# Four edits to a two-layer transformer kernel on one core: transposes one place later, masks later, x in pieces, last norm on three engines

## The reference

```python
u = rms_norm(h, norm_pre_mix[l]);  proj = u @ w_in[l]          # q_sb k_sb v_sb q_lat kv_lat k_r gate_logits
y_sb  = stick_breaking_attention(q_sb, k_sb, v_sb) @ w_o_sb[l]
y_mla = mla_attention(...) @ w_o_mla[l]                        # from q_lat, kv_lat, k_r
mixed = (g_sb * y_sb + g_mla * y_mla) @ w_out[l]               # g: sigmoid(gate_logits + b_gate)
h = h + rms_norm(mixed, norm_post_mix[l])
gu = rms_norm(h, norm_pre_ffn[l]) @ w_gate_up[l]
h = h + rms_norm((silu(g) * up) @ w_down[l], norm_post_ffn[l])
# second block, twice (attention, then retention):
x = layer_norm(ALPHA * x + y, ln_gain[i], ln_bias[i])          # (x - mu) * rsqrt(var + eps) * gain + bias
```

## Time and profile before

| | us |
|---|---|
| median of 3 runs (lowest, highest) | 2512.87 (2512.11, 2513.63) |
| the profiled execution | 2515.63 |
| its span, first to last instruction | 2513.8 |
| TensorE busy (share of the span) | 2483.7 (99%) |
| VectorE busy | 1531.8 (61%) |
| ScalarE busy | 1215.9 (48%) |
| GpSimd busy | 14.9 (1%) |

### The profile page before, as it was taken

The page is one execution under the profiler, slowest core; times in us unless marked ns, Lnnn a source line. Parts: engine busy times, 40 slices in busy tenths (PEclk is TensorE's granted clock), DMA queues, the critical chain, the costliest instruction groups (busy, mean ns, idle before and its releaser), DMA issues.

```text
span 2513.8 us, 33162 instructions
## 1 busy us (share of the span) xinstructions
PE 2483.7 (99%) x11514; PEld 2074.0 (83%) x11514; DVE 1531.8 (61%) x2132; ACT 1215.9 (48%) x1538; POOL 14.9 (1%) x29
## 2 busy tenths in 40 slices
PE   8999999999999999999999999999999999999997
PEld 7889888878888888888888888887888888888886
DVE  5557666565744454455556787668766566666557
ACT  5455776544644444444445445653544444444442
POOL 0000000000000000000000000000000000000000
PEclk9999999999999999999999999999999999999999
DMA  7566566775566666666567455455656556565663
GB/s 263 174 193 185 171 189 176 235 254 191 176 207 189 187 192 185 191 186 191 193 194 250 119 182 181 134 195 178 197 154 198 172 171 185 174 182 169 224 192 136
DMA packets 215026, 472.19 MB, mean 188 GB/s; under 512 B 14944, under 2 KB 24208, under 8 KB 213904
## 3 DMA queue, kind: packets, MB, share of 16 engines
q1 hardware_dynamic: 205968, 447.54, 58.1%
q10 hardware_dynamic: 6944, 12.86, 1.5%
q0 software_dynamic: 2016, 10.53, 1.2%
HBM read 464.57 MB, written 6.29 MB: 187 GB/s over the span
## 4 chain that ended last, share of the span: by engine, by line
PE 90%; DVE 4%; DMA 3%; ACT 2%; issue 1%; SPq 0%; ACTq 0%; DVEq 0%
PE acc L461 25%; PE acc L463 25%; PE acc L462 25%; PE aux L461 4%; PE aux L463 4%; PE aux L462 4%; PE aux L482 1%; ACT whi L1104 1%; DVE wlo L1721 1%; DMA raw<-w_in 1%; DMA raw<-w_o_sb 1%; DVE h L2385 0%; DMA raw<-r_w_out 0%; DMA raw<-w_out 0%; DVE stats L2379 0%
## 5 line engine op out<-in xcount | busy, mean ns | idle before, releaser
L1721 DVE TENSOR_TENSOR wlo<-raw,whi 128x1024 fp32r<-128x1024 f32 x823 | 1001.4, 1224 | 879.5 <-ACT whi L1104 877.2
L1104 ACT ACTIVATE whi<-raw 128x1024 fp32r<-128x1024 f32 x823 | 868.7, 1060 | 1129.1 <-PE acc L463 832.8
L461 PE MATMUL acc<-whi,xh 128*128 128x512 f32 (+1 forms) x2288 | 896.5, 392 | 1.7 <-DVE wlo L1795 1.1
L463 PE MATMUL acc<-whi,xl 128*128 128x512 f32 (+1 forms) x2288 | 889.7, 389 | 0.0
L462 PE MATMUL acc<-wlo,xh 128*128 128x512 f32 (+1 forms) x2288 | 889.2, 389 | 0.0
L463 PEld LDWEIGHTS acc<-whi,xl 128*128 128x128 f32 x2288 | 430.0, 188 | 88.4
L461 PEld LDWEIGHTS acc<-whi,xh 128*128 128x128 f32 x2288 | 430.4, 188 | 87.6 <-DVE xl L1791 1.8
L462 PEld LDWEIGHTS acc<-wlo,xh 128*128 128x128 f32 x2288 | 430.6, 188 | 83.5
L461 PE MATMUL acc<-whi,osh 128*128 128x512 f32 x400 | 155.9, 390 | 0.3 <-DVE osl L1731 0.2
L461 PE MATMUL aux<-whi,osh 128*128 128x512 f32 x400 | 156.0, 390 | 0.0
L463 PE MATMUL aux<-whi,osl 128*128 128x512 f32 x400 | 155.7, 389 | 0.0
(11 more groups left out here) (400 smaller groups left out, 1945.5 us busy)
## 6 DMA issues: line engine op xcount, KB each, us to landing
raw<-r_w_in SPq DMA_DIRECT2D x188, 512.0 KB, 3.7
raw<-w_gate_up SPq DMA_DIRECT2D x172, 512.0 KB, 3.6
raw<-w_in SPq DMA_DIRECT2D x112, 512.0 KB, 4.0
raw<-w_down SPq DMA_DIRECT2D x84, 512.0 KB, 4.6
raw<-a_w_in SPq DMA_DIRECT2D x76, 512.0 KB, 3.7
raw<-r_w_out SPq DMA_DIRECT2D x60, 512.0 KB, 4.6
raw<-w_out SPq DMA_DIRECT2D x28, 512.0 KB, 4.7
raw<-a_w_out SPq DMA_DIRECT2D x28, 512.0 KB, 4.0
```

The lines of the kernel that those rows point to most:

```text
L461: pe.matmul(dst, lh, rh, start=start, stop=False, skip_group_check=True)
L463: return pe.matmul(dst, ll, rh, start=False, stop=stop, skip_group_check=True)
L1104: A(whi[:, slot], raw[:, slot], ACT.Copy).then_inc(hi_done, 1)
L1721: V.tensor_tensor(wlo[:, slot], raw[:, slot], f32(whi[:, slot]), ALU.subtract).then_inc(lo_done, 1)
```

## The change

1. TensorE transposes the scaled first chunk behind u = 7 of the second chunk instead of u = 5; the copies into `qkT` on ScalarE and VectorE move likewise.
2. POOL fetches the masks when `used` is 16 instead of 4.
3. x goes into `h` in eight pieces of 256 KB, each when `used` has reached a further third unit of the second half of the gates, after `sb_y` is 4. `gbc1` waits for `used` to reach the first unit of `out`. VectorE waits for all eight pieces.
4. In the last layer norm, tile 0: VectorE copies its scale into `scale0` and goes on to tile 1; ScalarE multiplies the four pieces by it, and GpSimd adds the bias row to each. SP stores tile 0 by the new count `result0`.

```diff
+        scale0 = put("scale0", [P, 1], F32)
@@ sync
-                sp.wait_ge(sem("result"), n + 1)
+                sp.wait_ge(sem("result" if t else "result0"), n % 4 + 1)
@@ gpsimd
-            pool.wait_ge(used, 4)
+            pool.wait_ge(used, 16)
             bring("masks", [(mask_raw[:, 0:P], c_ntri), (mask_raw[:, P:2 * P], c_nones),
                             (mask_raw[:, 2 * P:5 * P], c_mask_sb), (mask_raw[:, 5 * P:9 * P], c_mask_mla)])
+            pool.wait_ge(sem("sb_y"), 4)
+            for n in range(8):
+                t, cols = n // 4, slice(n % 4 * CW, (n % 4 + 1) * CW)
+                pool.wait_ge(used, UNITS["gate"] + 32 + 3 * n)
+                pool.dma_start(h[:, t, cols], x[t * P:(t + 1) * P, cols]).then_inc(sem("x_again"), 16)
+
             pool.wait_ge(sem("dve_stage"), DVE_STAGE["mla_end"])
-            pool.dma_start(h[:], x.rearrange("(t p) n -> p t n", p=P)).then_inc(sem("x_again"), 16)
-
+            pool.wait_ge(used, UNITS["out"])
             bring("gains_in", [(gbc1[:], g_post_mix.partition_broadcast(P))])
...
+            pool.wait_ge(sem("gains_in"), 96)
+            for b in range(4):
+                cols = slice(b * CW, (b + 1) * CW)
+                pool.wait_ge(sem("scaled"), b + 1)
+                nc.gpsimd.tensor_tensor(h[:, 0, cols], h[:, 0, cols], lng2[:, 1, cols], ALU.add).then_inc(sem("result0"), 1)
@@ tensor
-                        if (c == 1 and u == 5) if first else u == 3:
+                        if (c == 1 and u == 7) if first else u == 3:
                             turned("qkv", i * 2 + c - 1)
                             turn_blocks(s0, 4).then_inc(sem("qkv_tr"), 1)
@@ scalar
-                        if c == 1 and u == 5 and first:
+                        if c == 1 and u == 7 and first:
                             cp("qkv", flat(qkT[:, 0:2]), aux[:, 0], 0)
...
+            act.wait_ge(sem("scale0_in"), 1)
+            for b in range(4):
+                cols = slice(b * CW, (b + 1) * CW)
+                A(h[:, 0, cols], h[:, 0, cols], ACT.Copy, scale=scale0[:]).then_inc(sem("scaled"), 1)
@@ vector
-                        if c == 1 and u == 5 and first:
+                        if c == 1 and u == 7 and first:
                             cp("qkv", flat(qkT[:, 2:4]), aux[:, 1], 0)
...
-            dve.wait_ge(sem("x_again"), 16)
+            dve.wait_ge(sem("x_again"), 16 * 8)
...
+                    if t == 0 and not name:
+                        V.tensor_copy(scale0[:], rs_y[:, 0:1]).then_inc(sem("scale0_in"), 1)
+                        continue
                     for b in range(4):
                         V.scalar_tensor_tensor(cols(h[:, t], b), cols(h[:, t], b), rs_y[:, t:t + 1], cols(tab[:, 1], b),
                                                ALU.mult, ALU.add).then_inc(sem(done), 1)
```

## The result

The changed kernel takes 2503.11 us (median of 6 executions, 2501.95 to 2505.81) against 2512.49 us of the kernel before on the same chip (2511.29 to 2514.79): ratio 0.9957, 95% interval 0.9947 to 0.9967, so 9.4 us faster (8.3 to 13.3). The profiled execution took 2502.06 us, its span 2500.3; before it was 2515.63 and 2513.8. Profile against profile the gain is 13.6 us, and 13.7 were forecast; median against median it is 9.4. So the mechanisms can be checked row by row, and the size has to be discussed.

A forecast was written before the change was run, and what follows sets the result against it. TensorE at a fixed pace bounds the kernel, so only its holes and VectorE's tail count. 7.7 + 4.3 + 1.7 = 13.7 us off the median 2512.87 gives 2499.2 us; range 2497.6 to 2503.6.

The forecast's parts named there:

- Part 1 and 2: End of chunk 2: transposes after units 14 and 15, masks later; unit 16 starts at 53.67 instead of 61.34, 7.7 us.
- the slow steps: TensorE's first matmuls behind a hole of some microseconds, nearly twice the pace: 0.44 us each behind the hole at 505.64.
- Part 3: Second mixing products: without x and gains transfers beside the weight loads, 2.77 us of waiting and 1.52 of slow matmuls vanish.
- Rival B: The hole at the mixing products stays in part; 1.4 to 4.3 us of gain lost, 2500.6 to 2503.5, chance 0.08.
- Part 4: Last norm: tile 0's products leave VectorE, tile 1's additions come earlier until bank 7 limits them; 1.7 us, not 2.5.
- Rivals C and D: Last norm: POOL's additions slow VectorE (4.4 us lost, chance 0.05); POOL sets the end, decisive from 2.7 us per addition (0.03).
- The sum: Whole kernel: 7.7 + 4.3 + 1.7 = 13.7 us off the profiled execution, 2515.63 becoming 2501.9.
- the same 13.7 off the median gives 2499.2: Whole kernel: the gain summed for the profiled execution also comes off the runs' median, 2512.87 us.
- lower bound of 2497.6: Bottom of the range: 1.62 us of mask shift instead of 1.4, unit 15 without its 0.2, spread of some 0.8.
- the first hole: TensorE's wait of 4.8 us before the transposes at the end of chunk 2, forecast to vanish.
- the forecast's own range: Whole kernel: 2498.4 to 2500.0 us if the forecast holds, chance 0.70.
- two holes: TensorE's waits before the chunk 2 transposes (4.8 us) and before the second mixing products (2.6 us), both forecast to go.

The follow-up runs named there:

- the gains early: The changed kernel with x still in pieces but the 1 MB gains row fetched at the end of MLA as before: 2503.23 us.
- the changed kernel again: The changed kernel, unaltered, run once more on another chip against the kernel before: 2502.35 us, ratio 0.9952.
- The parts alone: The kernel before with only the transposes moved, only x and gains transfers changed, or only the last norm on three engines: 2510.14, 2511.55 and 2514.07 us.
- 1.0 for the masks: The changed kernel with the masks fetched at 4 used units instead of 16: 2503.39 us, 1.0 more than the changed kernel beside it.

## Why the prediction was right, and where its size was off

**Part 1 and 2, forecast 7.7.** Right: 7.1 in the profile, 7.9 in the second profile of the changed kernel (61.34 - 53.48). The squares of x start 1.5 us earlier (1.4 forecast); unit 15 loses nothing. The 0.6 between 7.1 and 7.7 is a late TensorE, which the prediction didn't have: unit 14 starts at 47.99 instead of 47.13. The first product comes 0.2 us later than in the profile of before, the slow steps cost 1.2, and 0.55 of small waits in the next units are missing in return. Before, TensorE came early to the hole at 47 us anyway, and a delay of its start vanished in it.

**Part 3, forecast 4.3.** Right: no hole, no slow steps, the pieces free, the gains row free. Rival B has fallen. The loads came in 5.8 us, not 4 to 5, and the product with 3 us in hand, not 4.

**Part 4, forecast 1.7.** Right: 1.7 in the profiles (13.9 to 12.2), with bank 7 as the limit. Rivals C and D did not occur, but both are real: they are kept out by POOL being done at 2489.65, one microsecond before the first instruction with two SBUF operands (2490.71).

**The sum.** 7.1 + 4.3 + 1.7 and 0.5 in small waits elsewhere are the 13.6 us between the profiled executions, against 13.7. The step that failed is "the same 13.7 off the median gives 2499.2". The profiled execution of before was the slowest of its chip, 3.1 us above the final median of 2512.49, and the profiled one of the changed kernel was 1.05 below its own: 13.57 - 3.14 - 1.05 = 9.4. The prediction put the spread of executions at 0.8 us either side, from three of them; six on that chip lie 3.5 us apart and 33 on another 7.5. (Its lower bound of 2497.6 doesn't follow from its own terms either: 2499.2 - 0.2 - 0.2 - 0.8 is 2498.0.)

Part of the spread is shown. The slow steps behind a long hole vary: the first hole cost 5.6 to 7.1 us, and the prediction took them from an execution with ten. That is a mis-sized term of up to 1.5 us, 0.5 against the mean of the four. The start varies: in the eight profiles of the changed kernel and its variants unit 13 starts between 43.95 and 45.27, 1.3 us apart, and nothing hides that now. Two more places vary in all kernels alike, though no edit touches them. Behind the hole near 1745 us, which is about 3 us long in every profile, five profiles have no slow step and eight have some, among the transposes or the products behind them, which costs these 0.8 to 1.4 us. Here two executions, the changed kernel with the gains early and the changed kernel again:

```profile
1744.73 2.64 PE L502 MATMUL aux<-ident,h 128*128 128x128 f32 x16 [2.81 <-DVE h L2409]
1747.32 0.50 PE L473 MATMUL acc<-apart,xh 128*128 128x512 f32 x1
```

```profile
1745.27 3.10 PE L503 MATMUL aux<-ident,h 128*128 128x128 f32 x16 [2.79 <-DVE h L2410]
1748.02 0.78 PE L474 MATMUL acc<-apart,xh 128*128 128x512 f32 x1
```

And some 245 steps from 111 to 120 us on take 0.207 us in six profiles and 0.203 in the seven others, 1.0 us in all.

Which of the two medians is nearer to the usual gain isn't settled. On the three other chips the kernel before took 2515.25, 2514.66 and 2514.11 us; 2512.49, from six executions, is the lowest of its four medians. The changed kernel took 2503.11 and 2502.35. So most of what is missing at 9.4 lies in those six executions of before; whether this is the chip or chance stays open. The parts alone gave 5.1, 3.7 and 1.2 with 1.0 for the masks, 11.0 together, and 9.4 and 12.3 both lie within both intervals.

The range held by luck. It was made wide for lost terms, not for this: 2503.11 lies 0.5 us inside its upper bound and 3.1 outside the forecast's own range of 2498.4 to 2500.0, among the times of rivals B and C, neither of which occurred.

## What to carry to other kernels

Where one engine runs at a fixed pace, list the steps that are longer than the pace: two holes and the tail gave this change to within tenths between two profiles, while the engines' busy shares say nothing of it. Each hole costs its slow steps too, and their number differs from execution to execution: take them from several profiles, and don't set off a profiled execution against a median of others. Work given to POOL is cheap only while VectorE has no instruction with two SBUF operands.

## What the runs showed of the hardware

- Beside POOL's additions a product on VectorE of a single column, with two SBUF operands, took 1.2 us instead of 0.2: about a whole addition of POOL, whatever its own size. Instructions with one operand in PSUM kept their 0.69.
- In TensorE's stream steps of up to 1.4 us between starts, and one of 1.71, were followed by no slow step; those of 2.8 us and more at the two holes of the change by 2 to 10, at a granted clock of 0.56 to 0.79 in the stretch 52 to 59 us of two profiles. But behind steps of 2.9 to 3.1 us near 1745 us five profiles of thirteen had none: the clock from 1747 to 1752 us is 1.00 in one of these and 0.66 in the changed kernel's second profile.
- 1 MB of foreign transfers at the end of MLA was free, with 0.5 us in hand; 2 MB cost 1.5 us in the trace, 3 MB 4.0 to 4.6 in four profiles.
